# A two-block transformer kernel: the second block's attention scores as two fp32r passes, the rotary swap as DMAs, and the weight buffers rearranged

## What is computed

```
def apply_rope(x, cos, sin):                  # on every 64-wide head
    x1, x2 = split(x, 2, axis=-1)             # halves of 32
    return concat([x1 * c - x2 * s, x2 * c + x1 * s])

# second layer, differential attention: 8 heads of 2 x 64 channels
q, k, v = split(h @ w_qkv)
q, k = apply_rope(rms_norm(q)), apply_rope(rms_norm(k))
s = q . k / 8 (causal);  p = softmax(s);  a = p[0] - lam * p[1];  o = a @ v
x = x + (rms_norm(o) * 0.8) @ w_o;  x = x + swiglu(rms_norm(x))

# third layer, window of 128 with sinks: 16 query heads over 4 key heads
k, v = apply_rope(rms_norm(h @ w_k)), h @ w_v
q = apply_rope(rms_norm(h2 @ w_q))
s = q . k / 8 over 256 keys of a band, with one sink value per head
x = x + softmax(s) @ v @ w_o;  x = x + swiglu(rms_norm(x))
```

## Time and profile before

| what | value |
|---|---|
| median of the three executions | 2206.7 us |
| the profiled execution's own time | 2205.89 us |
| its span, first to last instruction | 2204.1 us |
| TensorE matmul (PE) busy | 2084.5 us, 95% of the span |
| weight load (PEld) busy | 1588.8 us, 72% |
| VectorE (DVE) busy | 1124.0 us, 51% |
| ScalarE (ACT) busy | 788.3 us, 36% |
| GpSimd (POOL) busy | 261.4 us, 12% |
| mean granted TensorE clock | 0.967 |
| DMA | 158.7 MB, 72 GB/s |

### The profile page before, as it was taken

One profiled execution on the slowest core, in us unless ns is written; L12 is line 12 of the kernel. 1 busy time (PEld: TensorE's weight loads), 2 busy tenths in 40 slices (PEclk: granted clock), 3 DMA queues, 4 the chain that ended last, 5 costly groups with the idle time before them and its releaser, 6 DMA issues.

```text
span 2204.1 us, 24397 instructions
## 1 busy us (share of the span) xinstructions
PE 2084.5 (95%) x9282; PEld 1588.8 (72%) x9282; DVE 1124.0 (51%) x2121; ACT 788.3 (36%) x1717; POOL 261.4 (12%) x210
## 2 busy tenths in 40 slices
PE   6989888799999999999998999999989989999999
PEld 4766666678888887755546788888766667888887
DVE  5554566654333336466646343433667765434433
ACT  3444444423222223335443322322345643323221
POOL 3000032221001012011102100101200011101000
PEclk9989998999999999989969999999989999999999
DMA  5211100023333323211102233332210112333332
GB/s 190 85 39 52 45 10 1 1 77 96 96 96 94 97 76 107 77 48 39 39 0 67 88 99 92 96 96 86 86 58 30 29 31 85 105 96 96 96 94 88
DMA packets 45619, 158.74 MB, mean 72 GB/s; under 512 B 5056, under 2 KB 5440, under 8 KB 45248
## 3 DMA queue, kind: packets, MB, share of 16 engines
q1 hardware_dynamic: 45504, 157.19, 23.6%
HBM read 155.07 MB, written 2.10 MB: 71 GB/s over the span
## 4 chain that ended last, share of the span: by engine, by line
PE 83%; DVE 9%; ACT 4%; issue 2%; DMA 1%; POOL 0%; SPq 0%; ACTq 0%; DVEq 0%
PE bank L731 22%; PE bank L733 21%; PE bank L732 21%; PE bank L839 5%; DVE WL L1288 2%; PE bank L882 2%; PE bank L840 1%; PE bank L752 1%; PE bank L706 1%; PE bank L707 1%; PE bank L708 1%; PE bank L926 1%; PE bank L758 1%; PE bank L906 1%; PE bank L915 1%
## 5 line engine op out<-in xcount | busy, mean ns | idle before, releaser
L1288 DVE TENSOR_TENSOR WL<-RAW,WH 128x512 fp32r<-128x512 f32 (+2 forms) x584 | 416.6, 752 | 126.5 <-ACT WH L1017 124.6
L731 PE MATMUL bank<-HH,WH 128*128 128x512 f32 x1056 | 432.7, 410 | 29.4 <-DVE WL L1288 20.0
L731 PE MATMUL bank<-GH,WH 128*128 128x512 f32 x1088 | 444.4, 408 | 6.4 <-DVE GL L1542 5.0
L1017 ACT ACTIVATE WH<-RAW 128x512 fp32r<-128x512 f32 (+2 forms) x584 | 329.2, 608 | 307.1 <-PE bank L733 177.2
L733 PE MATMUL bank<-GH,WL 128*128 128x512 f32 x1088 | 431.1, 396 | 0.0
L732 PE MATMUL bank<-GL,WH 128*128 128x512 f32 x1088 | 430.7, 396 | 0.0
L733 PE MATMUL bank<-HH,WL 128*128 128x512 f32 x1056 | 416.5, 394 | 0.0
L732 PE MATMUL bank<-HL,WH 128*128 128x512 f32 x1056 | 416.3, 394 | 0.0
L731 PEld LDWEIGHTS bank<-HH,WH 128*128 128x128 f32 x1056 | 201.4, 191 | 73.2 <-DVE WL L1288 22.3
L731 PEld LDWEIGHTS bank<-GH,WH 128*128 128x128 f32 x1088 | 205.7, 189 | 58.5 <-issue 7.4
L732 PEld LDWEIGHTS bank<-GL,WH 128*128 128x128 f32 x1088 | 205.7, 189 | 50.2 <-issue 4.8
(11 more groups left out here) (221 smaller groups left out, 2182.1 us busy)
## 6 DMA issues: line engine op xcount, KB each, us to landing
RAW<-in_wgu SPq DMA_DIRECT2D x132, 512.0 KB, 3.6
RAW<-in_wd SPq DMA_DIRECT2D x48, 512.0 KB, 3.6
RAW<-in_wd SPq DMA_DIRECT2D x24, 384.0 KB, 3.2
RAW<-in_da_qk SPq DMA_DIRECT2D x16, 512.0 KB, 3.6
RAW<-in_w_inh SPq DMA_DIRECT2D x12, 512.0 KB, 3.6
RAW<-in_w_in SPq DMA_DIRECT2D x8, 512.0 KB, 3.9
RAW<-in_w_out SPq DMA_DIRECT2D x8, 512.0 KB, 3.6
RAW<-in_da_v SPq DMA_DIRECT2D x8, 512.0 KB, 3.7
```

The costliest lines, as they stand in the source:

```text
L731: e.matmul(b, w_h, hi[st.x][k], start=(k == 0), stop=False)
L1017: e.activation(whs[s % NW][:, a:b], raw[s % NRAW][:, a:b], ACT.Copy).then_inc(S["wh"], 1)
L1288: e.tensor_tensor(wls[s % NW][:, a:b], raw[s % NRAW][:, a:b], whs[s % NW][:, a:b].bitcast(F), ALU.subtract).then_inc(S["wl"], 1)
```

## The change

It has five parts.

1. **Scores.** Rotated queries and keys are split into a high half (fp32r) and the rest. A query head becomes a 128-row tile with the high half in rows 0 to 63 and the low half in rows 64 to 127; a key head becomes two tiles, one with its high half in both row halves, one with its low half in both. A score is then two fp32r matmuls of 128 rows into the same bank, and the mask.
2. **Rotary swap.** The permutation matmul is gone. SP issues four DMAs of 32 partitions x 512 (64 KB each) per unit from TMP into a new TMP buffer (`swap`), and the sign is in the sine table. New steps: `swp` right after `qst`, `rot` five ticks later (DVE: multiply by the sine, add; ACT: round to the high half), `rlo` two ticks after that (DVE: subtract for the low half), then `stk`: SP issues the DMAs that stack the halves, of 64 partitions x 512 (128 KB) each, four for a query unit and eight for a key unit. POOL's product with the cosine stays. ACT's copies into KW are gone.
3. **Buffers and leads.** Stacked queries and keys have two buffers instead of four, so `stk` of a head waits until the scores of the head two before it are done. `DA_LEAD` is 40 instead of 64, and the gate is two heads ahead instead of three.
4. **Weights.** RAW and WL are one tensor of five buffers; the low half is written over the raw weights. SP loads unit s when PE is through with unit s-5, and loads are now steps of the plan, in one SP queue with `swp` and `stk`.
5. **Layout.** TMP has six tiles; constants lose the permutation matrix; the gains are padded from 473 to 480 columns. In the kernel before every tile's address is already a multiple of 64 bytes.

```
-DA_LEAD, SW_LEAD = 64, 20
+DA_LEAD, SW_LEAD = 40, 20
-NRAW, NW = 2, 4
+NR, NW = 5, 4
@@ fm and tm, after a unit's last tri
+                        put("ld", u + NR)
                         queue_split(u + NW)
@@ qk_norm
             now("qst", st, m)
             if rope:
-                later(5, lambda: put("qpm", st, m))
+                put("swp", st, m)
+                later(5, turn)
+        def turn():
+            put("rot", st, m)
+            later(2, split)
+        def split():
+            put("rlo", st, m)
+            stacks.append((st, m))
+            stack()
+    def stack():
+        while stacks:
+            st, m = stacks[0]
+            if st != "ks" and over[0] < (m // 2 if st == "qk" else m) - 1:
+                return
+            put("stk", *stacks.pop(0))
@@ the gate of the second layer
-    drive(state["att"], state["prj"], PROJ_PER_DA, lambda: state["first_over"] or cur[0] // 2 <= over[0] + 3)
+    drive(state["att"], state["prj"], PROJ_PER_DA, lambda: state["first_over"] or cur[0] // 2 <= over[0] + 2)
@@ SP
             def load(s):
-                if s >= NRAW:
-                    p.wait_ge(S["wl"], 2 * (s - NRAW + 1))
+                if s >= NR:
+                    p.wait_ge(S["unit"], s - NR + 1)
+            def swap(st, m):
+                g = NM[st] + m - 6
+                p.wait_ge(S[OUT[st]], m + 1)
+                if g >= 2:
+                    p.wait_ge(S[stacked(g - 2)[0]], stacked(g - 2)[1])
+                for a in range(0, 128, 32):
+                    b = a + 32 if a % 64 == 0 else a - 32
+                    e.dma_start(tmp[4 + m % 2][a:a + 32, :],
+                                tmp[2 + m % 2][b:b + 32, :]).then_inc(S[f"sw{m % 2}"], 16)
+            def stack(st, m):
+                p.wait_ge(S["nm_lo"], g + 1)
+                if st == "qk" and m >= 4:
+                    p.wait_ge(S["sc"], SC["d"] + 8 * (m // 2 - 1))
+                elif st == "sq" and m >= 2:
+                    p.wait_ge(S["sc"], SC["s"] + 8 * (m - 1))
...
@@ PE
-            def qpm(st, m):
-                norm_bank("nm_rm", g + 1)
-                e.matmul(nb, perm, tmp[2 + m % 2], start=True, stop=True).then_inc(S["nm_pm"], 1)
@@ scores
                 e.matmul(b[:, 0:n], lhs, rhs, start=True, stop=False, skip_group_check=True)
+                if rhs_lo is not None:
+                    e.matmul(b[:, 0:n], lhs, rhs_lo, start=False, stop=False, skip_group_check=True)
                 e.matmul(b[:, mcol:n], identb, mask, start=False, stop=True,
@@ ACT
+            def rot(st, m):
+                p.wait_ge(S["nm_q"], NM[st] + m - 6 + 1)
+                e.activation(nat_hi[m % 2], tmp[m % 2], ACT.Copy).then_inc(S["nm_hi"], 1)
@@ DVE
+            def rot(st, m):
+                c, s = tmp[m % 2], tmp[4 + m % 2]
+                p.wait_ge(S[f"sw{m % 2}"], 64 * (g // 2 + 1))
+                p.then(e.tensor_tensor(s, s, RSN[:, :], ALU.mult))
+                p.settle()
+                p.wait_ge(S["nm_cs"], g + 1)
+                e.tensor_tensor(c, c, s, ALU.add).then_inc(S["nm_q"], 1)
+            def rlo(st, m):
+                p.wait_ge(S["nm_hi"], g + 1)
+                e.tensor_tensor(nat_lo[m % 2], tmp[m % 2], nat_hi[m % 2].bitcast(F),
+                                ALU.subtract).then_inc(S["nm_lo"], 1)
```

More of the change, by code:

```diff
@@ L223, in plan @@
     state = {"prj": None, "att": None, "first_over": False}
-    over, cur = [0], [0]
+    over, cur, stacks = [0], [0], []
     def need(s):
@@ L823, in c_tp, with scores @@
                 done.then_inc(S["c_tp"], 1)
-            def scores(s, lhs, rhs, mask, mcol, n):
+            def scores(s, lhs, rhs, mask, mcol, n, rhs_lo=None):
                 b = scb[s % 3]
```

191 lines of the change are left out of this document (101 added, 90 removed).

## The result

| | median of | us | lowest to highest |
|---|---|---|---|
| before | 6 runs | 2203.6 | 2192.2 to 2208.0 |
| after | 6 runs | 2215.4 | 2211.6 to 2220.2 |
| after, the profiled execution | 1 | 2211.6 (span 2209.8) | |

A forecast was written before the change was run, and what follows sets the result against it. It took PE, busy 95% of the span, as the bound, with the lead turning latency-bound and DVE bounding the third layer's attention. Second layer -32 and third layer -15 gave 2205.9 - 47 = 2159 us, range 2140 to 2178 (chance 0.44).

The forecast's parts named there:

- Scores and permutation, work on PE: Second and third layers: cheaper scores take 22 and 19 us off PE's work, dropped permutations 14 and 9.
- The loads, the layout, the feed-forward parts: Whole kernel: weight loads stay hidden, tiles are aligned already, feed-forward stretches stay unchanged; 0 us.
- The lead (+5): Second layer before attention: units turn latency-bound at 10.3 us instead of 7.54, five units take 43 us instead of 38.
- The middle (+9): Second layer, projection interleaved with attention: swap hidden, 1.5 us of waits added per head over six heads, +9 us.
- of 10.3 us twice per head: Second layer's middle: the unit's chain through swap and rounding, twice per head, leaves under 2 us of play.
- 19.6 of 22: Second layer's middle: DVE's work per head, 19.6 us, set against PE's 22.0 us per head after the change.
- The tail (-10): Second layer's attention after the projection: 10 us come back of 31 us lost to the lower clock.
- the second stage's -32: Second layer's attention stage: PE work -36, lead +5, middle +9, tail -10, together -32 us.
- The third layer (-15): Third layer: -12 us in its attention, where DVE becomes the bound, and -3 us before it.
- What can go is the 13.3 us: Third layer's attention: of DVE's idle time only 13.3 us of waits for scores and two or three more can go.
- the slower one: Rival, second layer: swap lands late behind stacks, rot holds DVE, PE waits; decides from about 7 us, 2219 us; chance 0.08.
- The lower clock: Rival, second layer: emptier PE gets the lower clock; lead +13, tail's 10 not returned, middle +5; 2187 us; chance 0.21.

The follow-up runs named there:

- e2: Kernel after, with the turning step (sine product, sum, rounding) 7 ticks behind the swap instead of 5, behind the next unit's square on ScalarE; 2229.8 us.
- e12: Kernel after, with each swap issued as eight DMAs of 16 rows instead of four of 32, the same bytes; 2257.4 us.
- e3: Kernel after, with the swap DMAs undone and TensorE's permutation matmul back; stacks, fp32r passes, weights' buffers and layout stay; 2193.9 us.
- e8: Kernel after, with the permutation back on TensorE and the third layer's lead of 28 blocks and gate of 3 pairs; 2178.9 us.
- e10: e4 with the second block's queries and keys rounded to fp32r, one pass per score, low halves left out, no stacks or subtraction; 2165.4 us.
- e13: e8 with VectorE's product with the result of Ln and Exp one tick behind the scaling, no work changed; 2157.1 us.
- e6: Kernel before, with only the second layer's lead of 40 blocks instead of 64 and gate of 2 heads instead of 3; 2181.2 us.
- e7: Kernel after, with the third layer's lead of 28 blocks instead of 20 and gate of 3 pairs instead of 2; 2205.3 us.
- e5: Kernel after, with the stacking DMAs issued from GpSimd's queue instead of SyncE's, where swaps and weight loads stay; 2205.9 us.
- e4: Kernel after, with float32 scores as before, no stacks, rounding or subtraction; the swap by DMA, weights' buffers and layout stay; 2174.5 us.
- e16: Kernel before, with the second layer's lead of 40 and gate of 2, and VectorE's product one tick behind the scaling; 2174.6 us.
- e17: e13 with TensorE's permutation matmul one tick ahead of VectorE's sine product; 2145.1 us, ratio 0.9738.
- e11: Kernel after, with two of each swap's four DMAs issued by GpSimd's queue and two by SyncE's; 2210.6 us.

## Why the prediction was wrong

*Scores and permutation, work on PE.* Right: 0.32 and 0.55 us per score, and PE's busy time fell by 73 us, where 64 of work were forecast; what the other 9 are I did not take apart. *The loads, the layout, the feed-forward parts:* right, 0 as read from unchanged stretches; I ran no kernel with these parts alone.

*The lead (+5).* The mechanism was right, the size not: 11.4 to 12.0 us per unit instead of 10.3, +16.5 us by unit 120. "The first two units are not yet held back" failed: the first two steps from ones matmul to ones matmul took 12.0 and 11.5 us. The other terms that were mis-sized are the swap (3.9, or 4.5 behind stacks, for 3.5), its issue (0.61 for 0.45), and the ones matmul, which took 1.90 us for 1.12 when the clock fell.

*The middle (+9).* This is the step that failed: "The swap is hidden here, since five ticks with attention steps hold more DVE work than 3.5 us." The swap was hidden from DVE in part of the units only (it waited 6.8 us for DMAs in three of some eight units from 975 to 1085), and from ACT in none: its rounding waits for swap and sum, with the next square behind it. The chain that the forecast knew, "of 10.3 us twice per head", took 11 to 18 us per unit there, 15.3 in the mean over the three heads, so that heads came 29 to 32 us apart instead of 25; moving the turning step behind the square gave the second stage 16 us (e2), and lengthening the swap by 2.5 us cost 2.3 per unit (e12). The sum "19.6 of 22" failed with it: it adds up what each engine does and leaves out what an engine in order waits for. And of PE's 4.5 us per head the cheaper scores' 2.8 didn't come back as time at all (e3, e8 and e10, 83.6 to 84.5 us for three heads, 83.8 before); only with DVE's order changed too did a part of them (e13).

*The tail (-10).* Mis-sized. I took 10 of 31 us "between none and all"; from unit 130 to the end of the stage the kernel after needs 34.6 us less than before, and e6, with lead and gate alone, 30.1. It hid how dear the rest was: the second stage's -32 was -36 + 5 + 9 - 10 in the forecast, and is about -25 for lead and gate (e6), -3 for permuted, stacked scores (e3; as little as two traces of one kernel can differ by), and +23 for putting the swap in (after less e3; less e8 it is +17).

*The third layer (-15).* I let only the first stack delay a score; each pair's does, 14.1 us of waits in five places, worth 8 us with the swap (e7) and 19 without (e8). "DVE becomes its bound" was right in kind: with the stacks out of the way (e8) the stage stood at -2.4, and DVE's product one tick later brought it to -16.8 (e13), near the forecast -15. "What can go is the 13.3 us" was wrong: it took the waits for scores as the only ones of DVE that can go, and the one for Ln and Exp was worth as much.

*The rivals.* The sign was that of the slower one, which I gave 0.08: it had `rot` behind the swap hold an engine that PE waits for. But it named DVE and looked for a swap of 7 us behind stacks. The engine is ACT, whose order puts the next square behind `rot`, and a swap of 3.9 us is enough; the stacks ahead of swaps are worth 4 us (offsets) to 10 us (medians) in e5. So the sign was not foreseen for the right reason. The lower clock did spread, 0.85 in the lead. The Trainium skill ("TensorE: Matmul & The Clock Gate", Part 1, what's actually happening) says that the clock follows how busy PE has been. This case agrees in the lead (44.1 of 57 us busy at 0.85, and 57 of 57 at 1.00 before), but the share of busy time alone doesn't order the stretches: 0.91 at 40.1 of 51 us in e6's tail, 0.68 at 62.6 of 72 in the tail before.

## What to carry to other kernels

Don't call an engine that serves in order free because of its busy share; move one of its waits and measure. Once PE had less to do, the order of VectorE, busy 72% of the middle (78.7 of 110 us in e8), set the pace of both stages, and taking work from TensorE alone bought about a fifth of it (9 us of more than 41, e4 to e10). The reverse holds too: the same move in the kernel with PE full bought the heads nothing (e16). The Trainium skill ("Perfetto Trace Analysis", Identifying the Most-Contended Engine) would have VectorE judged by its occupancy; these runs do not bear that out, since moving VectorE's product, and then the matmul that it waits for, by one tick, with no work changed, gave 34 us (e8 to e17). And when a change puts a long wait on a chain, ask for every engine on it what is queued behind the waiting instruction; take a new lead or gate as a part with a price of its own, and measure it alone.

## What the runs showed of the hardware

The DMA issues of the kernel after, 903 to 1170 (count, KB each, median us to landing), and the stacks as GpSimd issues them in e5 (ns of an issue, min/median/max; then us to landing):

```profile
PR<-TMPR SPq DMA_DIRECT2D x96, 128.0 KB, 2.3
RAW<-in_da_qk SPq DMA_DIRECT2D x12, 512.0 KB, 3.7
TMP<-TMP SPq DMA_DIRECT2D x64, 64.0 KB, 2.0
```

```profile
L1804 POOL DMA_DIRECT2D PR<-TMPR x64: 516/523/555, 934.3 to 1122.5; - x64
...
DMA to landing us min/median/max: 2.2/2.8/5.5
```

Half the bytes land hardly sooner (2.0 us for 64 KB, 2.3 for 128), and an issue on SP costs 0.61 us for 32 rows and 0.62 for 16 (eight of them 4.96 us in e12): at these sizes a copy inside SBUF was priced by its count. The Trainium skill ("DMA: Bandwidth & Descriptors", Anatomy of one DMA, the gpsimd path) has about 50 ns for the sequencer's dispatch of a DMA that GpSimd issues, with the making of descriptors as a small item beside it; GpSimd's rows here show 0.52 us for a whole issue, ten times that, and don't part the two. Its stacks in e5 land after 2.8 us where SP's take 2.3, but in e11 the two queues share each swap and GpSimd's 64 KB land after 2.1 us, SP's after 2.5. And the first layer's length differed by 6 to 8 us between traces of kernels that are the same there, as much as the two profiled executions of before and after stand apart.
